# The taps of k's convolution next to each other in the order of a recurrent layer

## The chip, the cores and the metric

The kernel runs on one core of a Trainium2 chip. The metric is the device time of one execution in microseconds (us). Five engines work side by side, each through its own list of instructions in order: TensorE (PE) multiplies matrices, VectorE (DVE) and ScalarE (ACT) work on elements, GpSimd (POOL) does a few element operations here, and SyncE (SP) issues the DMAs. They meet by semaphores: an instruction that has to wait holds everything behind it on its engine.

## The reference, cut to what matters

The kernel computes two blocks; the change lies in the first, a gated delta net (the second, with attention and a recurrence of its own, follows it untouched) over 1024 tokens with 8 heads of q and k and 16 heads of v. A chunk is 64 tokens in the reference; the kernel uses 128.

```python
proj = h @ w_in
qkv, z, b_lin, a_lin = split(proj)
qkv = silu(causal_depthwise_conv(qkv, conv_w))          # 4 taps
q, k, v = split(qkv)
q, k = l2norm(q) * dh ** -0.5, l2norm(k)                 # each k head serves two v heads
...
a_mat = where(strict, (k * beta) @ k.T * decay, 0)       # in each chunk
t_mat = inverse(a_mat + eye)                             # triangular solve
...
def step(state, chunk):                                  # in order over the chunks
    v_new = u - w @ state
    o = q_dec @ state + qk @ v_new
    state = state * gl + k_dec.T @ v_new
```

## The kernel before

The stage works on one pair of v heads at a time (they share one head of q and k), pairs 0 to 7. `i` counts passes: pass `i` projects pair `i` and at the same time runs the solve and the recurrence of pair `i - 1`; pass 8 only finishes. In what follows, pair i means pass i.

**Jobs.** A job is one column block of 128 channels of the projection: 0 is q, 1 is k, 2 and 3 are the two v heads, 4 and above are gates z. A job has two halves of 512 tokens, each of eight slices, and a slice is three products on TensorE (lines 795 to 797: high weights by high and low inputs, low weights by high inputs). The first slice of a job waits until VectorE has written the low weights. The weights of a job come by one DMA into a single buffer (`w_raw`, line 497, SP); VectorE splits them by a cast to `w_hi` (line 942) and a subtraction to `w_lo` (line 944), in two buffers by turns. The next load into `w_raw` waits for that subtraction. The split for job j + 1 stands at the beginning of job j.

**Convolution and norm.** ScalarE copies a finished half out of PSUM (line 633, "evac"), applies the first tap (line 638), and VectorE adds taps 1 to 3, one instruction of 128 x 1024 each (line 962). Silu follows on ScalarE (line 703). For q and k the norm follows by halves: square on ScalarE (line 713), sum over channels as a product with ones on TensorE (line 827, "nsum"), Ln and Exp on ScalarE, and a multiplication on VectorE (line 1010).

**The solve.** The 32 x 32 blocks on the diagonal are inverted on VectorE in eight lane steps (lines 1081 and 1084, step 7 is followed by a turned copy, line 1088). SP writes the result out twice (lines 547 and 549), and reads it back in seven small DMAs (lines 558 and 561). Four merges then join the blocks on TensorE: the first at line 880, the second at lines 885 to 889, the third at 894 and the fourth at 899, with copies between them by ScalarE and VectorE (lines 1095, 1098, 1101, 1104). After the merges the recurrence goes through eight chunks of 128 tokens.

**The order.** `plan(i)` writes one list of steps by hand, and every engine walks through this list and takes from it what concerns it. The slices of TensorE are the clock of the list: `send(n)` puts the next n slices in. Work that follows a finished job is put into `behind` with a number: it goes into the list after so many further slices. When k's job (1) ends, its taps have the numbers 1 to 4, silu 15, the first square 17, the first sum 22. The split for the next job but one and the lane steps come in by themselves, at the slices where they stand. So between k's taps there stand, in every pair, the split for job 3, and in pairs 2, 4 and 6 also lane step 5, ahead of the last tap. In pairs 1, 3, 5 and 7 the next lane step stands behind the last tap.

SP walks through the same list: the load for job 4 stands behind the split for job 3, and in pairs 3, 5 and 7 the write of the lane result comes right after that load.

Of the kernel before, what the change touches and what calls it, by code (L numbers as in the profile page):

```python
# [222 lines left out]
def plan(i):  # L223
# [9 lines left out]
    out, behind = [], []  # L233
    sent = 0

    def finish(s):
        j, h = s[1:3]
        out.append(("evac", j, h))
        if h == 0:
            return  # L240
        if 0 <= j < N_CONV[i]:
            for q in range(TAPS):
                behind.append((1 + q, ("tap", j, q)))
            behind.append((15, ("silu", j)))
        else:
            out.append(("zstore", j))
        if j == 1 and N_CONV[i]:
            for m, (square, total, scale) in enumerate(((1, 5, 6), (7, 11, 14), (17, 22, 23), (24, 28, 30))):
                w = (m // 2, m % 2)
                behind.append((square, ("nsquare",) + w))  # L250
                behind.append((total, ("nsum",) + w))
                behind.append((scale, ("norm",) + w))

    def send(n):
        nonlocal sent, behind
        for _ in range(min(n, len(slices) - sent)):
            s = slices[sent]
            if s[2:] == (0, 1):
                out.append(("split", s[1]))
            elif s[2:] == (0, 2):  # L260
                out.append(("weights", s[1]))
            out.append(s)
            sent += 1
            behind = [(n - 1, x) for n, x in behind]
            out.extend(x for n, x in sorted(behind, key=lambda e: e[0]) if n <= 0)
            behind = [(n, x) for n, x in behind if n > 0]
            if s[3] == KD - 1:
                finish(s)
# [2555 lines left out]
```

## Time and profile before

| | |
|---|---|
| median of 3 runs | 2115.33 us (2114.32 to 2115.81) |
| profiled execution | 2121.64 us, its span 2119.8 us |
| TensorE busy in the span | 1991.9 us (94%) |
| VectorE | 1294.2 us (61%) |
| ScalarE | 864.7 us (41%) |
| mean granted clock of TensorE | 0.979 |

The span runs from the first to the last instruction of one profiled execution. The stage of the change lies between about 60 and 905 us of it. In a timeline each row is a start, a length, the engine and line, the operation, its output and inputs with their shapes, how many instructions of the kind stand together, and, in brackets, how long the engine was idle just before and what ended that. VectorE's share of 61% is a mean over the program; in the lane steps it is far higher.

### The profile page before, as it was taken

The page shows a single profiled execution, that of the slowest core. Times are in us where ns is not written, and L with a number is a line of the kernel's source. Part 1 is how long each engine was busy: PE and PEld are TensorE (multiplying, and loading weights), DVE is VectorE, ACT ScalarE, POOL GpSimd, SP SyncE. Part 2 cuts the span into 40 slices and gives each one's busy share as a digit, 9 for nine tenths or more (in the row PEclk, how much of TensorE's full clock was granted, in tenths as well). Part 3 has the DMA queues.
Part 4 walks back from the last instruction along what each step waited for, and adds up shares of the span by engine and source line. Part 5 has one row for each costly group of instructions (what it writes and reads, how often), then busy time and mean ns, then how long its engine had stood idle before and what let it go on. Part 6 is the DMA issues. An engine that isn't in the chain of part 4 may idle for free. (4 is left out here: it accounts for less than half of the span.)

```text
span 2119.8 us, 29549 instructions
## 1 busy us (share of the span) xinstructions
PE 1991.9 (94%) x11256; PEld 1635.2 (77%) x11256; DVE 1294.2 (61%) x2447; ACT 864.7 (41%) x1392; POOL 136.9 (6%) x114
## 2 busy tenths in 40 slices
PE   4989999999999999969998999999999899999998
PEld 2667878888887878857776787787787788888877
DVE  6776778796869696659435645454464445733543
ACT  5644353534445353159203244435443337600221
POOL 0020202111120202000000000000000000000000
PEclk8999999999999999989999999999999999999999
DMA  7222323232324233458113220311313116211232
GB/s 280 84 75 69 95 79 105 66 99 74 107 64 112 71 114 96 140 178 282 55 41 127 75 80 27 104 60 50 100 40 100 53 70 225 80 50 50 80 119 80
DMA packets 130251, 204.47 MB, mean 96 GB/s; under 512 B 56852, under 2 KB 88340, under 8 KB 129088
## 3 DMA queue, kind: packets, MB, share of 16 engines
q1 hardware_dynamic: 130112, 202.58, 29.8%
q8 instruction: 91, 1.49, 0.3%
q14 instruction: 48, 0.39, 0.1%
HBM read 156.22 MB, written 42.11 MB: 94 GB/s over the span
## 5 line engine op out<-in xcount | busy, mean ns | idle before, releaser
L795 PE MATMUL p_job<-h_hi,w_hi 128*128 128x512 f32 x768 | 322.3, 420 | 18.5 <-DVE h_lo L185 17.1
L797 PE MATMUL p_job<-h_hi,w_lo 128*128 128x512 f32 x768 | 303.0, 395 | 0.0
L796 PE MATMUL p_job<-h_lo,w_hi 128*128 128x512 f32 x768 | 302.7, 394 | 0.0
L1708 PE MATMUL m_job<-h_hi,m_hi 128*128 128x512 f32 x576 | 247.4, 429 | 5.0 <-issue 4.2
L1710 PE MATMUL m_job<-h_hi,m_lo 128*128 128x512 f32 x576 | 229.6, 399 | 0.0
L1709 PE MATMUL m_job<-h_lo,m_hi 128*128 128x512 f32 x576 | 228.9, 397 | 0.0
L795 PEld LDWEIGHTS p_job<-h_hi,w_hi 128*128 128x128 f32 x768 | 146.3, 190 | 59.3 <-issue 16.2
L796 PEld LDWEIGHTS p_job<-h_lo,w_hi 128*128 128x128 f32 x768 | 146.4, 191 | 35.0 <-issue 7.6
L797 PEld LDWEIGHTS p_job<-h_hi,w_lo 128*128 128x128 f32 x768 | 146.0, 190 | 31.6
L1708 PEld LDWEIGHTS m_job<-h_hi,m_hi 128*128 128x128 f32 x576 | 110.8, 192 | 25.6 <-issue 5.6
L633 ACT ACTIVATE pre<-p_job 128x512 f32<-128x512 f32 x96 | 56.7, 591 | 180.2 <-PE p_job L797 178.5
L1710 PEld LDWEIGHTS m_job<-h_hi,m_lo 128*128 128x128 f32 x576 | 109.9, 191 | 25.2
L1709 PEld LDWEIGHTS m_job<-h_lo,m_hi 128*128 128x128 f32 x576 | 111.0, 193 | 15.4
L2421 PE MATMUL e_b<-h_hi,m_hi 128*128 128x512 f32 x256 | 99.8, 390 | 0.8 <-ACT m_gt L1780 0.8
L2422 PE MATMUL e_b<-h_lo,m_hi 128*128 128x512 f32 x256 | 99.7, 389 | 0.0
L2423 PE MATMUL e_b<-h_hi,m_lo 128*128 128x512 f32 x256 | 99.7, 389 | 0.0
L962 DVE SCALAR_TENSOR_TENSOR qv<-pre,conv_w,qv 128x1024 f32<-128x1024 f32 x72 | 93.3, 1296 | 5.3 <-ACT qv L638 3.6
L1084 DVE TENSOR_TENSOR UL<-UL,lane_tmp 64x31 f32<-64x31 f32 (+15 forms) x248 | 83.0, 335 | 8.5
L1081 DVE TENSOR_TENSOR lane_tmp<-UL,AL 64x31 f32<-64x31 f32 (+15 forms) x248 | 82.7, 334 | 7.5
L608 POOL TENSOR_TENSOR gam<-gam,tri 128x512 f32<-128x512 f32 x32 | 41.7, 1303 | 516.1 <-DVE gam L1019 516.1
L1126 DVE SCALAR_TENSOR_TENSOR S<-S,gl,p_head 128x128 f32<-128x128 f32 x128 | 38.9, 345 | 52.1 <-PE p_head L929 52.1
L2135 DVE CUSTOM_DVE_ANT_0 sc<-p_sc,alibi 128x512 f32<-128x512 f32 (+3 forms) x96 | 49.5, 553 | 28.1 <-PE p_sc L1968 28.0
(399 smaller groups left out, 4232.9 us busy)
## 6 DMA issues: line engine op xcount, KB each, us to landing
w_raw<-in_w SPq DMA_DIRECT2D x49, 512.0 KB
m_raw<-in_w SPq DMA_DIRECT2D x49, 512.0 KB, 4.2
rows<-grows SPq DMA_DIRECT2D x32, 512.0 KB, 6.5
ada<-in_ada_w SPq DMA_DIRECT2D x8, 1024.0 KB, 5.3
z_scr<-pre SPq DMA_DIRECT2D x16, 512.0 KB, 2.7
o_scr<-oT SPq DMA_DIRECT2D x64, 128.0 KB, 1.8
ob<-o_scr SPq DMA_DIRECT2D x16, 512.0 KB, 5.0
zb<-z_scr SPq DMA_DIRECT2D x16, 512.0 KB, 4.9
```

The costliest lines, as they stand in the source:

```text
L795: nc.tensor.matmul(bank, hi, h_hi[:, k, cut], start=(k == 0), stop=False)
L796: nc.tensor.matmul(bank, hi, h_lo[:, k, cut], start=False, stop=False)
L797: last = nc.tensor.matmul(bank, lo, h_hi[:, k, cut], start=False, stop=(k == KD - 1))
L962: nc.vector.scalar_tensor_tensor(dst, pre[:, job(i, j) % 2, q:q + T], w, dst, ALU.mult, ALU.add).then_inc(conv_step, 1)
L1081: nc.vector.tensor_tensor(step, bc(UL[0:LANES, 0:r, j], 2, w), bc(AL[0:LANES, j, r:], 1, r), ALU.mult).then_inc(lane_done, 1)
L1084: nc.vector.tensor_tensor(UL[0:LANES, 0:r, r:], UL[0:LANES, 0:r, r:], step, ALU.subtract).then_inc(lane_done, 1)
L1708: nc.tensor.matmul(bank, hi, h_hi[:, k, cut], start=(k == 0), stop=False)
L1709: nc.tensor.matmul(bank, hi, h_lo[:, k, cut], start=False, stop=False)
L1710: last = nc.tensor.matmul(bank, lo, h_hi[:, k, cut], start=False, stop=(k == KD - 1))
L2421: nc.tensor.matmul(bank, hi, hi_rhs, start=first, stop=False)
L2422: nc.tensor.matmul(bank, hi, lo_rhs, start=False, stop=False)
L2423: return nc.tensor.matmul(bank, lo, hi_rhs, start=False, stop=final)
```

## The change

The number of slices after which a tap of k comes is 1 for all four taps, and no longer 1, 2, 3 and 4. Other jobs keep theirs. Steps with the same number keep the order in which they were put in.

```diff
         if 0 <= j < N_CONV[i]:
             for q in range(TAPS):
-                behind.append((1 + q, ("tap", j, q)))
+                behind.append((1 if j == 1 else 1 + q, ("tap", j, q)))
             behind.append((15, ("silu", j)))
```

In the list this reads as follows, here for pair 2 (slices are left out; tap 0 and the square are ScalarE's, the weights step is SP's load):

```
before: tap(1,0) nsquare(0,0) split(2) tap(1,1) weights(2) tap(1,2) lane(5) tap(1,3) nsum(0,0)
after:  tap(1,0) tap(1,1) tap(1,2) tap(1,3) nsquare(0,0) split(2) weights(2) lane(5) nsum(0,0)
```

`split(2)` is the step at job 2's beginning, which splits the weights of job 3. In pairs 0, 1, 3, 5 and 7 the list changes in the same way but for the lane step, which keeps its place behind the taps or ahead of them. No engine's work changes, only VectorE's order, in pairs 0 to 7.

## Rows read from the trace of the kernel before

**Rows 1.** Waits of TensorE, 60 to 905 us: in all, times, longest (us).

```profile
PE p_pre L827 <- ACT PM L713: 9.1, 5, 4.1
PE p_both L880 <- issue: 6.0, 2, 5.1
...
PE p_both L894 <- DVE U L1098: 1.2, 3, 0.4
```

**Rows 2.** Timeline of ScalarE, pair 2: start, length (us), instruction, idle before and releaser.

```profile
275.06 1.28 ACT L703 ACT_TABLE_LOAD   x1
280.31 1.06 ACT L703 ACTIVATE kT<-kT 128x1024 f32<-128x1024 f32 x1 [3.96 <-DVE kT L962]
```

**Rows 3.** Timeline of VectorE, pair 2.

```profile
271.50 0.68 DVE L942 CAST w_hi<-w_raw 128x1024 fp32r<-128x1024 f32 x1
272.21 1.23 DVE L944 TENSOR_TENSOR w_lo<-w_raw,w_hi 128x1024 fp32r<-128x1024 f32 x1
273.36 2.60 DVE L962 SCALAR_TENSOR_TENSOR kT<-pre,conv_w,kT 128x1024 f32<-128x1024 f32 x2
...
279.00 1.27 DVE L962 SCALAR_TENSOR_TENSOR kT<-pre,conv_w,kT 128x1024 f32<-128x1024 f32 x1
...
300.03 0.70 DVE L1095 COPY PM<-p_both 32x512 f32<-32x512 f32 x1
```

**Rows 4.** Windows: length, busy us (instructions) of PE, PEld, DVE, ACT, POOL; clock, DMA, GB/s.

```profile
255.00:300.70 45.70, 44.33 (x246) 34.63 (x244) 43.74 (x76) 25.29 (x32) 0.62 (x1) 1.00 0.40 114
```

**Rows 5.** Timeline of TensorE, pair 2.

```profile
276.81 0.39 PE L795 MATMUL p_job<-h_hi,w_hi 128*128 128x512 f32 x1
...
282.42 1.13 PE L827 MATMUL p_pre<-PM,ones 128*128 128x512 f32 x2 [1.37 <-ACT PM L713]
...
300.83 0.19 PE L885 MATMUL p_turn<-PM,U 32*32 32x32 f32 x1
```

**Rows 6.** Timeline of VectorE, pair 3.

```profile
376.98 1.23 DVE L944 TENSOR_TENSOR w_lo<-w_raw,w_hi 128x1024 fp32r<-128x1024 f32 x1
378.12 3.92 DVE L962 SCALAR_TENSOR_TENSOR kT<-pre,conv_w,kT 128x1024 f32<-128x1024 f32 x3
381.96 0.23 DVE L1081 TENSOR_TENSOR lane_tmp<-UL,AL 64x87 f32<-64x87 f32 x1
...
395.06 0.70 DVE L1095 COPY PM<-p_both 32x512 f32<-32x512 f32 x1 [1.03 <-PE p_both L880]
...
401.61 0.69 DVE L1098 TENSOR_SCALAR U<-p_both 32x512 f32<-32x512 f32 x1
```

**Rows 7.** Timeline of TensorE, pair 3.

```profile
381.08 0.39 PE L795 MATMUL p_job<-h_hi,w_hi 128*128 128x512 f32 x1
...
393.81 1.20 PE L880 MATMUL p_both<-TD,at 32*32 32x32 f32 x64
...
402.45 0.76 PE L894 MATMUL p_both<-TD,at 64*64 64x64 f32 x10 [0.41 <-DVE U L1098]
```

**Rows 8.** Timelines of VectorE and TensorE, pair 0: a product behind its weights.

```profile
82.30 1.22 DVE L944 TENSOR_TENSOR w_lo<-w_raw,w_hi 128x1024 fp32r<-128x1024 f32 x1
...
83.58 0.50 PE L795 MATMUL p_job<-h_hi,w_hi 128*128 128x512 f32 x1 [0.68 <-DVE w_lo L944]
```

**Rows 9.** Timeline of SP, pair 3: DMAs as issued.

```profile
378.23 0.33 SPq L497 DMA_DIRECT2D w_raw<-in_w  x1
383.47 0.47 SPq L547 DMA_DIRECT2D u_lanes<-UL  x1
...
389.13 2.08 SPq L561 DMA_DIRECT2D U<-u_lanes  x4
```

**Rows 10.** The reads of the lane result (line 561), issue to landing.

```profile
DMA to landing us min/median/max: 2.1/2.5/3.7
```

**Rows 11.** The reads of the turned lane result (line 558), issue to landing.

```profile
DMA to landing us min/median/max: 1.8/2.3/4.0
```

## The prediction

> **What bounds the kernel now.** I first read the waits of TensorE over the stage (60 to 905 us). In all eight head pairs TensorE is nearly always at work, so the change can only matter where TensorE waits, or where it would begin to. Four kinds of wait bear on it [rows 1]. The sum of squares of the norm (line 827) waited for ScalarE's square five times, 9.1 us in all: 4.1 and 0.9 us in pair 0 and 1.37 us in each of pairs 2, 4 and 6 [rows 5]. The first merge (line 880) waited 5.1 us once, in pair 1. The third merge (line 894) waited 0.4 us in each of pairs 3, 5 and 7. And the first product of a job has waited for VectorE's low half of the weights (line 944) before, 0.68 us at 83.58 [rows 8].
>
> Next, ScalarE's timeline in pair 2 shows why the sum of squares is late there: k's silu stood idle 3.96 us behind VectorE's last tap of k [rows 2]. VectorE's timeline of that pair shows the reason [rows 3]: two taps, then lane step 5, and only then the third tap, at 279.00. So k's taps are the chain that releases line 827 in the even pairs, and this is what the change speeds up.
>
> The question is whether TensorE profits, and for that I read VectorE between the lane steps and the merges. In the stretch up to the first merge's copy it is busy 43.74 of 45.70 us with 76 instructions [rows 4]; the 1.96 us left are 0.026 us for each instruction, the small gaps between dependent ones, and no wait is among them (the same holds in pairs 4 and 6, 43.1 of 45.0 and 43.6 of 45.6). The copy of the first merge ends at 300.03 + 0.70 = 300.73 [rows 3], and the second merge starts on TensorE at 300.83 [rows 5]. In the even pairs VectorE, not TensorE, sets when the second merge starts.
>
> **The change, part by part.** No instruction is added or removed. ScalarE, TensorE, GpSimd and SP keep their order. On VectorE alone, in pairs 0 to 7, the three taps of k pass ahead of the split of job 3's weights (cast and subtraction) and, in pairs 2, 4, 6, the third tap also passes lane step 5. SP's next weight load (for job 4) waits for that split, so it moves with it.
>
> *Taps, even pairs.* The taps can start at 271.50, where the split starts now, and end 3.92 us later [rows 3, 6] at 275.42 in place of 280.27. Silu's table load ends at 275.06 + 1.28 = 276.34 [rows 2], so silu runs to 277.4 and the 1.37 us wait at 282.42 [rows 5] goes.
>
> *Split, all pairs.* It starts later by three chained taps less the 0.08 us by which an independent neighbour starts early (378.12 + 3.92 = 382.04, but the lane step stands at 381.96 [rows 6]): 3.84 us. Job 3's first slice on TensorE waits for it. In pair 3 the subtraction ends at 376.98 + 1.23 = 378.21 and the first slice starts at 381.08 [rows 6, 7]: 2.87 us of slack (it is the product that stands six slices of three ahead of k's first sum of squares). Pairs 5 and 7 repeat the two rows, 2.88 and 2.87 us apart. After the change the subtraction ends at 382.05. From the end of a subtraction to the product that waits for it the trace has 83.58 - (82.30 + 1.22) = 0.06 us [rows 8]. So TensorE starts at 382.11 and loses 1.03 us, a wait that is not there now. What hid the split was just this slack, and 3.84 us is more than 2.87.
>
> In the even pairs the same sum gives 272.21 + 1.23 + 3.84 + 0.06 = 277.34 against 276.81 [rows 3, 5]: 0.53 us lost, ahead of a wait of 1.37 us that is gone, so TensorE is 0.84 us ahead at line 827. In pair 1 the same two rows are 3.27 us apart: 3.84 + 0.06 - 3.27 = 0.63 us are lost, and swallowed by the 5.1 us wait at the first merge, whose data come from the lane steps; those keep their place in pair 1. In pair 0 the same two rows leave 7.0 us, more than 3.84, and the rest of that pair waits for the broadcast rows from memory: nothing.
>
> *Does the loss in pairs 3, 5, 7 stay?* From the first slice to the first merge TensorE runs without a gap (the merge starts at 393.81 [rows 7]). VectorE then waits 1.03 us for that merge, and from there copy, split, three taps and the second merge's copy stand end to end up to 401.61 + 0.69 = 402.30 [rows 6], for which TensorE waits another 0.41 us [rows 7]. All of this begins with the first merge, so it moves by the full 1.03 us and gives nothing back: 3 x 1.03 = 3.09 us.
>
> *Does the gain in pairs 2, 4, 6 stay?* TensorE arrives 0.84 us earlier at the second merge, and VectorE's copy ends when it did, because the sum of its work is the same. The gain turns into a wait there. VectorE's own sum grows a little: a dependent tap starts 0.04 us after its forerunner (3 x 1.28 + 2 x 0.04 = 3.92), an independent neighbour 0.08 us before its forerunner ends, and one junction of the second kind becomes one of the first: 0.12 us each, 3 x 0.12 = 0.36 us lost. Bounds for the even pairs: -0.84 (all kept) to +0.12 each; I take +0.12, since the two rows that meet at 300.73 and 300.83 say that VectorE ends last.
>
> The Trainium skill (VectorE: DVE Perf Modes, The DRAIN you can't avoid) says that a Vector instruction does not start until the one before has emptied its pipe. By that the order would not matter and the 0.36 us would fall away (2118.4 us). The trace disagrees: the neighbours overlap by 0.08 us [rows 6].
>
> *The moved weight load.* In pair 3 it is issued at 378.23, and the lane steps' result is written at 383.47 [rows 9]. 3.84 us later the load starts at 382.07, 1.40 us ahead of that write, and the two share the DMA engines. The write, the 7 reads back (the last four issued from 389.13 on, the last at 390.7) and the merge follow. A read lands 2.1 to 3.7 us after its issue, 2.5 in the median [rows 10], so about 393.2; the merge started at 393.81, so that 0.5 us are free now (never under zero), and TensorE comes 1.03 us later. A delay under 1.5 us costs nothing. Price of such a delay from the rows: the reads of the other lane copy land 1.8 us after issue at best, 4.0 at worst [rows 11], and the even pairs issue a weight load right ahead of them; so a load 0.6 us ahead costs at most 2.2 us, and one 1.40 us ahead at most 2.2 - 0.8 = 1.4 us. Value taken: 0, with ends 0 and, if the whole 2.2 us fell on the write, 0.7 us per odd pair. VectorE's next split needs that load too; up to 1.5 us of delay there are covered by the 1.03 us wait ahead of 395.06 [rows 6], which itself moves 1.03 us later.
>
> **The sum.** 3.09 + 0.36 = +3.45 us on the profiled execution's 2121.64 us (2119.8 of span and 1.8 around it). That execution lies 0.3% above the median of the runs; the waits are the same in kind, so I carry the difference over: 2115.33 + 3.45 = 2118.8 us.
>
> The clock does not come in: it was granted in full (1.00, 2.4 GHz) throughout the stretch that holds one of the 1.37 us waits [rows 4], and the new waits are shorter.
>
> **Rivals.** *The moved load decides (slower).* Mechanism: in pairs 3, 5, 7 the 512 KB load stands in the queue ahead of the lane steps' write and the first merge waits for its data instead of for TensorE. It decides from a delay of 1.5 us; at 2.2 us it costs 0.7 us more in each of the three: 2118.8 + 2.1 = 2120.9. Against it: the load has 1.40 us start. For it: the landing times scatter by 1.6 to 2.2 us, and one engine that is late holds the whole transfer. The Trainium skill (DMA: Bandwidth & Descriptors, Queues, rings and completion order) says that SP owns one ring on each of the 16 engines and that each ring is worked off in order. By that the write stands behind the whole load, which is this rival; the reads landing at 4.0 instead of 1.8 us agree.
>
> *The even pairs keep their gain.* If VectorE were not last at the second merge, -0.84 x 3 instead of +0.36: 2118.8 - 2.9 = 2115.9, no change. Against it: the 0.1 us between the copy's end and the merge.
>
> *The weights come in time (faster).* If the first slice did not have to wait, because VectorE gets to the taps earlier than the trace says, the even pairs would gain 1.37 x 3 = 4.1 us and the odd lose nothing: 2111.2. It needs both, so little speaks for it.
>
> *Nothing moves.* The 1.03 us are given back later in the stage: 2115.3. The 0.41 us wait at the third merge is no such place, as shown.
>
> **How the numbers follow.** Forecast 0.55; load decides 0.25; even pairs keep the gain 0.09; nothing moves 0.06; faster 0.05. A measurement of this kernel can tell 0.2% (4.2 us) from no change, so slower begins at 2119.6, faster at 2111.1. The forecast itself (+3.45, with a scatter of 1 us) puts some 0.12 of its 0.55 past that line, the load rival 0.2 of its 0.25: slower 0.32, faster 0.04, within 0.64. The range runs from the two no-change rivals (2115.3, rounded down for the runs' own spread of 1.5 us) to the load rival with a microsecond on top: 2114.9 to 2121.9. The forecast's own range is 2117.6 to 2119.8.
>
> **What would show it.** Right: in pairs 3, 5, 7 a new wait of about 1.0 us of line 795 for VectorE's line 944, with half of that in 1, 2, 4, 6; line 827's waits down from 9.1 to about 5 us; waits of some 0.8 us at the second merge (line 885) for line 1095 in 2, 4, 6; every later pair shifted. Wrong: no wait for line 944, a second merge in pair 2 that starts before 300.7, or a wait of more than 0.3 us at line 880 in pairs 3, 5, 7, which would make the load the cause.

## The result, and the profile after

| | kernel before | kernel after |
|---|---|---|
| median of 6 runs each | 2115.57 us (2111.87 to 2117.93) | 2123.11 us (2119.24 to 2125.76) |
| ratio, 95% interval | | 1.0036 [1.0022, 1.0050] |
| profiled execution, its span | 2121.64 us, 2119.8 us | 2119.24 us, 2117.4 us |
| TensorE, VectorE busy | 1991.9, 1294.2 us | 1988.0, 1294.4 us |
| mean granted clock | 0.979 | 0.982 |

In these runs the changed kernel is slower, and its 2123.11 us lie above the predicted range (2114.9 to 2121.9). The two profiled executions say the opposite (2117.4 us of span after, 2119.8 before), so spans can't be compared here; the stage has to be read place by place.

The waits of TensorE from 60 to 905 us, after (columns as in [rows 1]):

```profile
PE p_job L795 <- DVE w_lo L944: 5.6, 9, 0.9
PE p_pre L827 <- ACT PM L713: 5.5, 2, 4.1
PE p_both L880 <- issue: 5.1, 3, 3.2
...
PE p_turn L885 <- issue: 2.5, 3, 1.1
...
PE p_both L894 <- DVE U L1098: 1.2, 3, 0.4
```

Against [rows 1], line 827's three waits of 1.37 us are gone (9.1 to 5.5 us), and two kinds of wait have come: line 795 for VectorE's low weights, and line 885, the second merge.

Pair 3 shows the first. VectorE's timeline there, to be held against [rows 6]:

```profile
372.92 3.91 DVE L962 SCALAR_TENSOR_TENSOR kT<-pre,conv_w,kT 128x1024 f32<-128x1024 f32 x3
376.75 0.69 DVE L942 CAST w_hi<-w_raw 128x1024 fp32r<-128x1024 f32 x1
377.47 1.23 DVE L944 TENSOR_TENSOR w_lo<-w_raw,w_hi 128x1024 fp32r<-128x1024 f32 x1
378.62 0.23 DVE L1081 TENSOR_TENSOR lane_tmp<-UL,AL 64x87 f32<-64x87 f32 x1
...
392.87 0.70 DVE L1095 COPY PM<-p_both 32x512 f32<-32x512 f32 x1 [1.03 <-PE p_both L880]
```

TensorE's timeline of the same pair, against [rows 7]:

```profile
377.49 0.39 PE L797 MATMUL p_job<-h_hi,w_lo 128*128 128x512 f32 x1
378.75 0.50 PE L795 MATMUL p_job<-h_hi,w_hi 128*128 128x512 f32 x1 [0.88 <-DVE w_lo L944]
379.09 0.39 PE L796 MATMUL p_job<-h_lo,w_hi 128*128 128x512 f32 x1
...
400.25 0.53 PE L894 MATMUL p_both<-TD,at 64*64 64x64 f32 x6 [0.41 <-DVE U L1098]
```

The taps come first, the subtraction ends at 377.47 + 1.23 = 378.70, and job 3's first slice starts at 378.75. Without a wait it would have followed the product at 377.49 by 0.23 us, at 377.71 (from unrounded times), so its start is 1.04 us late. VectorE's 1.03 us before line 1095 and TensorE's 0.41 us before line 894 stand unchanged: nothing behind has taken the loss up.

Pair 2, TensorE's timeline after, against [rows 5]:

```profile
273.85 0.50 PE L795 MATMUL p_job<-h_hi,w_hi 128*128 128x512 f32 x1 [0.38 <-DVE w_lo L944]
...
278.11 1.02 PE L827 MATMUL p_pre<-PM,ones 128*128 128x512 f32 x2
...
297.52 0.18 PE L885 MATMUL p_turn<-PM,U 32*32 32x32 f32 x1 [1.03 <-issue]
```

Line 827 no longer waits, and the 1.03 us at the second merge take what was won. VectorE's timeline says for what it waited:

```profile
296.72 0.70 DVE L1095 COPY PM<-p_both 32x512 f32<-32x512 f32 x1
```

The copy ends at 297.42, and the merge starts 0.10 us later, as before [rows 3, 5]. The same 0.10 us lie between the two in pairs 4 and 6, before and after.

### The profile page after: what moved, and what is told of

It reads as the page before. It is cut to its first block and busy times, and to the rows that moved or that the text cites. A ratio compares the mean times of both kernels' runs of the same rounds, so it can differ in the third digit from the quotient of the medians.

```text
span 2117.4 us, 29549 instructions
## 1 busy us (share of the span) xinstructions
PE 1988.0 (94%) x11256; PEld 1630.5 (77%) x11256; DVE 1294.4 (61%) x2447; ACT 864.9 (41%) x1392; POOL 137.0 (6%) x114
## 3 DMA queue, kind: packets, MB, share of 16 engines
q8 instruction: 91, 1.49, 0.3%
```

## The experiments

All comparisons with repeated rounds are against the kernel before on the same chip. The runs of a kernel scatter by up to 14 us, so beside the times I compare the traces pair by pair: in each trace I take the start of the fifth slice of k's job in every pair and the time from there to the next pair's (for pair 7, to the fifth slice of the second job of pass 8), and subtract the same time in the trace of before. The last column is the sum over pairs 2 to 7.

```
kernel     pair 0    1 |    2     3     4     5     6     7 |  2 to 7
after      -0.43 -0.63 | 0.13  1.17  0.49  1.13  0.13  1.23 |   4.29
c1_again   -0.87  0.07 | 0.15  1.13  0.57  1.13  0.11  1.19 |   4.27
c1_odd      1.70  0.52 |-0.02  1.16  0.21  1.15 -0.03  1.21 |   3.67
c1_even     1.47 -1.52 | 0.11 -0.02  0.32  0.01  0.09  0.01 |   0.53
c1_third   -1.81 -0.39 | 0.13 -0.02  2.34  0.01  0.09  0.01 |   2.56
c2_two      0.18 -0.53 |-0.03 -0.03  0.05 -0.02 -0.05  0.13 |   0.05
c2_free     1.91  0.59 |-0.77 -0.02  0.54 -0.02 -1.23 -0.02 |  -1.52
c2_best     0.16 -0.70 |-0.50 -0.48 -0.12 -0.49 -0.85 -0.43 |  -2.88
c2_null    -0.87 -0.27 | 0.00 -0.02  0.06  0.00 -0.09  0.01 |  -0.04
```

c2_null is the kernel before once more: pairs 2 to 7 repeat within 0.1 us, pairs 0 and 1 do not (in pair 1 the first merge waits for the lane data, 3.2 to 5.1 us in the ten traces). A difference of 0.1 us in a pair can therefore be read, although one of 4 us in a single total can't.

The experiments change the one line of the diff, and two of them the list behind it:

```diff
c1_odd:   behind.append((1 if j == 1 and i in (3, 5, 7) else 1 + q, ("tap", j, q)))
c1_even:  behind.append((1 if j == 1 and i in (2, 4, 6) else 1 + q, ("tap", j, q)))
c1_third: behind.append((min(1 + q, 3) if j == 1 and i in (2, 4, 6) else 1 + q, ("tap", j, q)))
c2_two:   behind.append(((1, 1, 1, 4)[q] if j == 1 and i in (3, 5, 7) else 1 + q, ("tap", j, q)))
```

**The change again.** No edit; the same kernel in more runs, to size it.

> The changed kernel once more, with more runs, to settle its size. Theory W (job 3's first slice waits for the weights that VectorE now splits 3.84 us later; VectorE sets the second merge in the even pairs): from the profiles, +1.17 us in each of pairs 3, 5, 7 and +0.15 to +0.5 us in each of 2, 4, 6, so +4.3 us (ratio 1.0020) and a wait of line 795 for line 944 of 0.88 us in the odd and 0.4 us in the even pairs. Theory D (the moved weight load holds up the lane steps' write, unseen in the one profiled execution): +7.5 us (1.0036) again, and a wait of line 880 in odd pairs in this profile. Theory N (the rest is scatter of the clock outside the stage): near +4 us, with no new wait.

Measured: 2121.53 us (12 runs) against 2118.48 us (35 runs), ratio 1.0012 [0.9999, 1.0024]. The pairs repeat those of the first trace within 0.1 us. What differs between the two comparisons (1.0036 and 1.0012) lies outside these pairs, and most of it in the kernel before: its median was 2115.57 there and is 2118.48 here.

**Only pairs 3, 5, 7.**

> The change in pairs 3, 5 and 7 alone. Theory W: three waits for line 944 of 0.88 us and +3.5 us (1.0016); the three waits of 1.37 us at line 827 in the even pairs stay. Theory D: +5 to +7 us (1.0024 to 1.0033), since the moved load meets the lane steps' write in these pairs alone.

Measured: 2121.37 us, 1.0020 [1.0007, 1.0033]. The three pairs lose 1.16, 1.15 and 1.21 us, the even ones nothing but 0.2 us in pair 4. This part of the change carries 3.5 of the 4.3 us. TensorE's waits from 240 to 905 us:

```profile
PE p_pre L827 <- ACT PM L713: 4.1, 3, 1.4
PE p_job L795 <- DVE w_lo L944: 2.6, 3, 0.9
```

Line 827's waits in the even pairs are all still there; the three waits for the split are those of the odd pairs.

**Only pairs 2, 4, 6.**

> The change in pairs 2, 4 and 6 alone. Theory W: the 1.37 us waits at line 827 go, waits of 0.4 us for line 944 and of 0.4 to 1.1 us at the merges (lines 880 and 885) come, +0.3 to +0.8 us (1.0001 to 1.0004). Rival (the even pairs keep their gain): -2.5 us (0.9988).

Measured: 2119.83 us, 1.0010 [0.9998, 1.0021]. The pairs lose 0.11, 0.32 and 0.09 us. Line 827's 4.1 us are gone from the stage and the kernel isn't faster: the gain is swallowed at the merges.

**Only the third tap, in pairs 2, 4, 6.** The split stays where it was; only the last tap passes lane step 5, which is enough for silu to come in time.

> In pairs 2, 4 and 6 the third tap alone passes lane step 5; the split of the weights stays where it was, all other pairs are as before. Theory W: no wait for line 944 and none of 1.37 us at line 827, but TensorE then waits some 1.3 us at the merges, because VectorE's copy (line 1095) ends no sooner: +0.1 to +0.5 us. Rival (line 827 is what the even pairs wait for): -4.1 us (0.9981).

Measured: 2120.5 us, 1.0005 [0.9992, 1.0019]. There is no wait for the split, so TensorE has the whole 1.37 us in hand, and pairs 2 and 6 still lose 0.13 and 0.09 us. TensorE's timeline in pair 2:

```profile
291.73 1.20 PE L880 MATMUL p_both<-TD,at 32*32 32x32 f32 x64 [0.68 <-issue]
...
296.97 0.18 PE L885 MATMUL p_turn<-PM,U 32*32 32x32 f32 x1 [1.08 <-issue]
```

The two merges take it all back. Pair 4 was not expected: it lost 2.34 us. Its first merge, and the stretch behind it (window columns as in [rows 4]):

```profile
490.02 1.28 PE L880 MATMUL p_both<-TD,at 32*32 32x32 f32 x64 [2.47 <-issue]
```
```profile
480.00:490.00 10.00, 7.55 (x34) 5.93 (x33) 9.15 (x9) 5.33 (x7) 0.00 (x0) 1.00 0.61 128
490.00:494.00 4.00, 3.98 (x71) 3.36 (x72) 3.90 (x6) 0.59 (x1) 0.46 (x1) 0.62 0.37 126
```

The lane data were read back late: SP's timeline has the four reads of line 561 issued over 4.59 us, where pair 2 of the same trace has 2.56 us.

```profile
286.80 2.56 SPq L561 DMA_DIRECT2D U<-u_lanes  x4
...
483.30 4.59 SPq L561 DMA_DIRECT2D U<-u_lanes  x4
```

The last of the four, issued at 487.40, landed 2.42 us later at 489.82, and the merge starts 0.20 us behind that. TensorE stood for 2.47 us, and then the granted clock fell to a mean of 0.62 over 4 us (products of 0.63 us in place of 0.39), which is the lower level of 1.2 GHz for most of it. In the two traces of the change, in c1_odd and in c1_even pair 4 loses 0.2 to 0.6 us.

**A shift that fits the slack.** In pairs 3, 5 and 7 two taps of k pass the split and the third stays behind it. The split then moves by 1.28 + 1.32 - 0.08 = 2.52 us, less than the 2.87 us that were free.

> In pairs 3, 5 and 7 two of k's three taps pass the split of job 3's weights, the third stands behind it; all else as before. The split then comes 1.28 + 1.32 - 0.08 = 2.52 us later, under the 2.87 us that the first slice leaves. Theory W (the wait for the weights is the price, and it has a threshold): no wait for line 944 in these pairs, each pair within 0.1 us of before, 0 us. Rival (any delay of the weights' split or of the weight load behind it costs in proportion): 2.52 / 3.84 of the 1.17 us that each pair lost with three taps, so 0.77 us each and +2.3 us.

Measured: 2119.02 us, 0.9999 [0.9988, 1.0010]; the three pairs change by -0.03, -0.02 and 0.13 us (the last is just over the 0.1 us that was expected). VectorE's and TensorE's timelines in pair 3:

```profile
373.82 2.59 DVE L962 SCALAR_TENSOR_TENSOR kT<-pre,conv_w,kT 128x1024 f32<-128x1024 f32 x2
376.33 0.69 DVE L942 CAST w_hi<-w_raw 128x1024 fp32r<-128x1024 f32 x1
377.05 1.23 DVE L944 TENSOR_TENSOR w_lo<-w_raw,w_hi 128x1024 fp32r<-128x1024 f32 x1
```
```profile
378.60 0.39 PE L795 MATMUL p_job<-h_hi,w_hi 128*128 128x512 f32 x1
```

The subtraction ends at 378.28 and the slice starts at 378.60, without a wait. The loss is no cost per tap that is moved: none is seen while the shift stays inside the slack.

**The gain set free.** If VectorE's copy for the second merge holds the even pairs, work that stands ahead of it and isn't urgent has to go behind it. c1_third's line, and at the end of the plan:

```diff
+    def behind_of(step, mark):
+        out.remove(step)
+        out.insert(out.index(mark) + 1, step)
+
+    if i in (2, 4, 6):
+        behind_of(("tap", 3, 3), ("merge", 0))
+        behind_of(("decay", i, 0), ("merge", 1))
```

> As c1_third (in pairs 2, 4 and 6 the third tap of k alone passes lane step 5), and in these pairs two things that stand ahead of VectorE's first merge copy (line 1095) go behind it: the third tap of job 3 to behind the first merge, the first decay step behind the second merge. Theory W (VectorE's copy is what swallowed the even pairs' gain): the copy ends some 2 us sooner, the second merge is set by TensorE, and 0.9 to 1.2 us of the 1.37 us stay in each pair: -2.7 to -3.6 us (0.9983 to 0.9987). Rival (the lane steps' data at line 880 hold TensorE up anyway): 0 to -1 us, with waits of about 1.3 us at line 880.

Measured: 2117.04 us, 0.9991 [0.9981, 1.0001]. Pairs 2 and 6 gain 0.77 and 1.23 us, pair 4 loses 0.54. The sum over the pairs, -1.5 us, lies between what theory W and its rival expected. The second merge no longer waits, where c1_third had two waits of some 1 us at line 885. Line 880 (887 in this kernel) waits for lane data as it did there. c1_third, then c2_free:

```profile
PE p_both L880 <- issue: 5.0, 4, 2.5
PE p_turn L885 <- issue: 2.0, 2, 1.1
```
```profile
PE p_both L887 <- issue: 5.0, 4, 2.2
```

So there were two holds: VectorE's order at the second merge, which this edit takes away, and the transfer of the lane data at the first, which stays and keeps the rest of the gain.

**Both kinds of pair.** c2_free, and in pairs 3, 5 and 7 the same for the third merge, whose wait of 0.41 us [rows 7] had the last tap of job 3 ahead of its copy:

```diff
+    if i in (3, 5, 7):
+        behind_of(("tap", 3, 3), ("merge", 1))
```

> As c2_free, and in pairs 3, 5 and 7 the third tap of job 3 goes behind the second merge, so that the copy for which the third merge waits (line 1098) comes 1.28 us sooner. Theory W: the three waits of 0.41 us at line 894 go as well, -1.2 us on top of c2_free, -3.9 to -4.8 us (0.9977 to 0.9982). Rival: the waits move to the fourth merge or to silu of job 3, and nothing more is won than with c2_free.

Measured: 2114.58 us (11 runs), 0.9985 [0.9975, 0.9995], faster than the kernel before by its interval, and 7 us under the changed kernel's 2121.53 us (measured on another chip; before had a median of 2118.48 us on both). By its ratio and by the sum over the pairs (-2.9 us) it falls short of the -3.9 to -4.8 us expected. All six pairs gain, the odd ones 0.48, 0.49 and 0.43 us, as expected, and the waits at the third merge are gone; pairs 2 and 6 gain 0.50 and 0.85 us, less than in c2_free, and still wait for lane data. VectorE's timeline in pair 2 shows the copy (line 1104 here) ahead of the last tap:

```profile
292.07 2.60 DVE L971 SCALAR_TENSOR_TENSOR qv<-pre,conv_w,qv 128x1024 f32<-128x1024 f32 x2
294.71 0.70 DVE L1104 COPY PM<-p_both 32x512 f32<-32x512 f32 x1
295.43 1.29 DVE L971 SCALAR_TENSOR_TENSOR qv<-pre,conv_w,qv 128x1024 f32<-128x1024 f32 x1
```

**The kernel before, once more.** No edit; for the scatter of a pair.

> The kernel before once more, for a second profile: how much of the difference of one pair between two traces is scatter. Theory W and theory N (scatter outside the stage): pairs 2 to 7 within 0.1 us of the first trace but for pair 4, where three other kernels lie 0.2 us and more above it; differences of some us in pairs 0 and 1 and behind the stage, where the clock changes.

Measured: 2115.81 us, and the last line of the table. Pair 4 repeats too (0.06 us).

## Why the prediction was right and wrong

**Its mechanism held, step by step.** The split moved past the 2.87 us of slack. The prediction had the first slice 1.03 us late; it is 1.04 us late. The wait for line 944 stands in six pairs from 240 us on (0.88 us in the odd, 0.38 in the even), line 827's waits fell to 5.5 us, line 885 waits 1.03 us, and line 1095 sets its end. c1_odd, c1_even and c2_two confirm it one by one: the odd pairs lose, the even ones win nothing, and while the split keeps inside its slack no pair's difference exceeds 0.13 us.

**The step that failed** is the last one: "the waits are the same in kind, so I carry the difference over: 2115.33 + 3.45 = 2118.8 us", and with it the range, which allowed for "the runs' own spread of 1.5 us" and no more. Three runs of before from 2114.32 to 2115.81 were taken for the kernel's time and scatter. In the later comparisons the same kernel ran 64 times: mean 2118.5 us, standard deviation 3.0, from 2111.33 to 2126.36. The three runs lay 3.1 us low and close together. I take that as chance; it isn't shown, since the granted clock of the first comparison's six runs of before (mean 2115.3 us) is not on record. 2118.5 + 4.3 = 2122.8 us, and the mean of 18 runs of the changed kernel is 2122.3. The profiled execution of before, 2121.64 us, was the hint: I read 0.3% as an oddity of that one execution, and it was the scatter.

**The other part is the size of the difference**: 4.3 us over pairs 2 to 7 in both traces, where I had 3.45. The term "3 x 1.03 = 3.09" measured 1.17 + 1.13 + 1.23 = 3.53. The late start is 1.04 us as worked out; what I left out is the restart. The first product after a wait lasts 0.50 us instead of 0.39, and its successor starts 0.34 us behind it instead of 0.23. I had used the row that shows this [rows 8] for another number and didn't price it. The term "3 x 0.12 = 0.36" measured 0.13 + 0.49 + 0.13 = 0.75: right in pairs 2 and 6, and in pair 4 something that I had no term for. There TensorE came to the first merge ahead of the lane data, in the changed kernel's trace:

```profile
490.95 1.20 PE L880 MATMUL p_both<-TD,at 32*32 32x32 f32 x64 [1.03 <-issue]
```

Before, this merge had no wait. In c1_third it is 2.47 us and in c2_free 2.20. In c1_third's pair 4 SP issued the reads over a longer time, as shown above; why it does stays open.

**The order's own price.** Pairs 2 and 6 lost 0.09 to 0.15 us in four traces (the change twice, c1_even, c1_third), which fits the 0.12 us of one junction between neighbours turned from independent to dependent. The Trainium skill (VectorE: DVE Perf Modes, The DRAIN you can't avoid) says that the next instruction waits until the pipe has emptied; by that nothing would have been lost here, and the traces disagree. The section adds an exception, which I had passed over: a next instruction that nothing holds starts earlier. The overlap of 0.08 us [rows 6] agrees with that.

**The rivals.** *The moved load decides*: in pairs 3, 5 and 7 no wait appeared at line 880, so it did not. The delay it rests on is real. Issue to landing of the two writes of the lane result, lines 547 and 549, in the changed kernel:

```profile
DMA to landing us min/median/max: 2.9/2.9/3.8
...
DMA to landing us min/median/max: 3.0/3.0/3.6
```

Before, the maxima were 2.9 and 3.0. SP's timeline shows the load close ahead of both, against [rows 9]:

```profile
378.73 0.33 SPq L497 DMA_DIRECT2D w_raw<-in_w  x1
380.12 0.47 SPq L547 DMA_DIRECT2D u_lanes<-UL  x1
381.27 0.47 SPq L549 DMA_DIRECT2D t_lanes<-AL  x1
```

With a load 1.39 us ahead the first write lands 0.7 to 1.0 us later in pairs 3, 5 and 7, and the second, behind that late write, 0.6 us later. In c2_two the load is issued 2.60 us ahead of the first write, and the writes land as they did before (2.9 and 3.0 us). The room at the merge was somewhat less than the prediction's 1.5 us: in before the last read of pair 3, issued at 390.73, landed 2.7 us later, at 393.4, and not at 393.2. It was enough. The Trainium skill (DMA: Bandwidth & Descriptors, Queues, rings and completion order) has descriptors taken up in ring order on each engine, though a later one may finish first; a write that lands later behind a load agrees with that, in direction and not in the price I had feared. *The even pairs keep their gain* fell with c1_even and c1_third. *The weights come in time* fell with the 0.88 us wait. *Nothing moves* fell with the pairs that follow, none of which gives the loss back.

**The clock.** "The clock does not come in" holds for the change: in the stage from 240 to 905 us it is 1.00 before and after. It does come in for the total, since most of the scatter goes with it. The first row is the stage in before. The second is a stretch behind the stage in before, and the last the same stretch, with the same 353 products, in c1_again, whose run was 4.7 us faster (2116.91 us) although it holds the slower code:

```profile
240.00:905.00 665.00, 656.80 (x4829) 553.77 (x4828) 514.31 (x1027) 280.76 (x470) 96.64 (x79) 1.00 0.32 95
...
1273.10:1345.30 72.20, 69.96 (x353) 57.75 (x352) 34.09 (x86) 32.59 (x57) 0.00 (x0) 0.98 0.13 44
```
```profile
1273.30:1343.90 70.60, 68.38 (x353) 56.52 (x352) 34.03 (x86) 32.51 (x57) 0.00 (x0) 1.00 0.14 45
```

The same work takes 1.6 us less at the full clock. From the table's last mark (845 us in before) to the end, c1_again is 7.2 us faster than before in all, which more than hides the 4.3 us that it loses in pairs 2 to 7. Over the 64 runs of before, time and mean granted clock correlate at -0.77. A line through the runs of all kernels gives -1.49 us for +0.001 of mean clock. With that taken out, the differences to before (with one standard error) are +4.4 ± 0.8 us for the first six runs of the change and +4.3 ± 0.6 for the later twelve, both held against the 64 later runs of before, +3.6 ± 0.6 for c1_odd, +1.6 ± 0.6 for c1_even, +0.6 ± 0.6 for c1_third, 0.0 ± 0.6 for c2_two, -1.4 ± 0.6 for c2_free and -3.8 ± 0.6 for c2_best. These agree with the sums over the pairs within two standard errors, but for c1_third, where the sum of 2.56 holds one late read in one execution. The change's cost is thus 4.3 us, some 0.20%. The first comparison gave 0.36% (7.5 us between the medians); the other 3 us lie in its six runs of before, which were that much faster than the 64 later ones. That the clock made them faster is likely and not shown.

## What to carry to other kernels

In an in-order queue, look at every neighbour that a step is moved past and at the slack of the engine that waits for it: 3.84 us against 2.87 us decided this change, and 2.52 us cost nothing. A wait that goes is worth nothing as long as another engine ends last a little later; take what stands ahead of that engine's copy out of its way, and expect another hold (here a transfer) right beside it. Before you put a number on a total, ask how far runs scatter and with what: three runs that lie close together don't show it, and a stage compared place by place tells a tenth of a microsecond where totals don't tell four.

## What the runs showed of the hardware

The same kernel ran from 2111.33 to 2126.36 us in 64 runs. Their mean granted clock (0.977 to 0.984) goes with most of that, at a correlation of -0.77. A wait of TensorE cost more than its length: the second product after it started 0.34 us behind the first, in place of 0.23, which is 0.11 us for the restart, whether the wait was 0.38 or 0.88 us. The clock stayed at 1.00 after waits of 0.4 to 1.1 us, and after one of 2.20 us in c2_free; it fell to the lower level after the one of 2.47 us in c1_third. The first write of the lane result landed 3.6 to 3.9 us after its issue when a 512 KB load was issued 1.39 us ahead of it (the changed kernel), and after 2.9 us when the load was 2.60 us ahead (c2_two).
